# Weight differences made ahead of the join, all low halves of the last projection on VectorE, and a new order of its seven products

## What is computed

```
def conv_glu_ffn(h_norm, w_in, conv_w, conv_b, w_out):
    gate, up = jnp.split(h_norm @ w_in, 2, axis=-1)
    S = gate.shape[1]
    padded = jnp.pad(gate, ((0, 0), (CONV_WIDTH - 1, 0), (0, 0)))
    conv = conv_b
    for t in range(CONV_WIDTH):
        conv = conv + padded[:, t:t + S, :] * conv_w[t]
    return (jax.nn.silu(conv) * up) @ w_out
...
        h = h + conv_glu_ffn(rms_norm(h, norm_ffn[l]), w_ffn_in[l], ffn_conv_w[l], ffn_conv_b[l], w_ffn_out[l])
```

## Time and profile before

| | us |
|---|---|
| median of 3 runs (lowest, highest) | 1416.52 (1416.09, 1418.0) |
| the profiled execution: its time, and its span | 1415.03, 1413.3 |
| PE busy of the span | 1388.4 (98%) |
| DVE, POOL, ACT busy | 879.0, 666.3, 648.7 |
| mean granted clock of TensorE | 0.998 of full speed |

### The profile page before, as it was taken

The page is one execution under the profiler, slowest core; times in us unless marked ns, Lnnn a source line. Parts: engine busy times, 40 slices in busy tenths (PEclk is TensorE's granted clock), DMA queues, the critical chain, the costliest instruction groups (busy, mean ns, idle before and its releaser), DMA issues.

```text
span 1413.3 us, 17598 instructions
## 1 busy us (share of the span) xinstructions
PE 1388.4 (98%) x6797; PEld 1135.6 (80%) x6797; DVE 879.0 (62%) x1249; ACT 648.7 (46%) x1109; POOL 666.3 (47%) x365
## 2 busy tenths in 40 slices
PE   8999999999999999999999999999999999999998
PEld 6888778887788888888888887788777878887886
DVE  4584674665776206663265656836658895888687
ACT  6747583665332212322346555735753333334333
POOL 5645663542444344444346367535344434443542
PEclk9999999999999999999999999999999999999999
DMA  6332012331233233333333210223223602530521
GB/s 175 98 99 64 27 46 75 113 111 50 86 104 105 97 92 104 96 90 98 96 90 103 86 61 16 76 71 109 90 66 91 209 24 60 181 117 1 157 67 59
DMA packets 176305, 125.67 MB, mean 89 GB/s; under 512 B 14657, under 2 KB 152672, under 8 KB 176224
## 3 DMA queue, kind: packets, MB, share of 16 engines
q1 hardware_dynamic: 175664, 124.55, 29.4%
q10 hardware_dynamic: 560, 0.01, 0.0%
HBM read 122.44 MB, written 2.10 MB: 88 GB/s over the span
## 4 chain that ended last, share of the span: by engine, by line
PE 88%; DVE 8%; ACT 1%; issue 1%; DMA 1%; SPq 0%; DVEq 0%; ACTq 0%
PE bank L751 25%; PE bank L755 25%; PE bank L753 25%; PE bank L925 2%; DVE h L1912 1%; PE bank L1054 1%; PE bank L1055 1%; PE bank L1134 1%; PE bank L913 1%; PE bank L1094 1%; DVE w_lo L1919 1%; DMA raw<-in_w_ffn_in 1%; DVE Q L2108 1%; PE bank L1209 1%; DVE h_tok L1886 1%
## 5 line engine op out<-in xcount | busy, mean ns | idle before, releaser
L674 POOL TENSOR_TENSOR w_lo<-raw,w_hi 128x1024 fp32r<-128x1024 f32 (+2 forms) x206 | 495.0, 2408 | 596.0 <-ACT w_hi L1334 594.2
L751 PE MATMUL bank<-x_hi,w_hi 128*128 128x512 f32 x944 | 371.5, 394 | 3.8 <-issue 2.5
L755 PE MATMUL bank<-x_hi,w_lo 128*128 128x512 f32 x944 | 367.6, 389 | 0.0
L753 PE MATMUL bank<-x_lo,w_hi 128*128 128x512 f32 x944 | 367.5, 389 | 0.0
L1334 ACT ACTIVATE w_hi<-raw 128x1024 fp32r<-128x1024 f32 (+2 forms) x205 | 212.9, 1040 | 245.4 <-PE bank L755 236.9
L751 PEld LDWEIGHTS bank<-x_hi,w_hi 128*128 128x128 f32 x944 | 177.3, 188 | 47.2 <-issue 7.8
L753 PEld LDWEIGHTS bank<-x_lo,w_hi 128*128 128x128 f32 x944 | 177.3, 188 | 37.6 <-issue 1.4
L755 PEld LDWEIGHTS bank<-x_hi,w_lo 128*128 128x128 f32 x944 | 177.2, 188 | 36.9
L2226 DVE SCALAR_TENSOR_TENSOR conv<-gate_in,gains_all,conv 128x512 f32<-128x512 f32 x44 | 113.4, 2577 | 1.6
L1685 ACT ACTIVATE conv_silu<-conv 128x512 f32<-128x512 f32 x44 | 27.8, 632 | 176.5 <-DVE conv L2227 176.5
L1867 DVE TENSOR_TENSOR h<-h,bank 128x512 f32<-128x512 f32 x48 | 31.8, 681 | 105.3 <-PE bank L755 105.2
(11 more groups left out here) (341 smaller groups left out, 2484.8 us busy)
## 6 DMA issues: line engine op xcount, KB each, us to landing
raw<-in_w_ffn_in SPq DMA_DIRECT2D x88, 512.0 KB, 3.9
raw<-in_w_in SPq DMA_DIRECT2D x27, 512.0 KB, 3.7
raw<-in_w_ffn_out SPq DMA_DIRECT2D x20, 512.0 KB, 3.6
raw<-in_w_mix_out SPq DMA_DIRECT2D x16, 512.0 KB, 3.8
raw<-in_w_ca_kv SPq DMA_DIRECT2D x32, 256.0 KB, 3.2
raw<-in_w_ca_q SPq DMA_DIRECT2D x8, 512.0 KB, 3.4
raw<-in_w_ca_out SPq DMA_DIRECT2D x8, 512.0 KB, 3.9
raw<-in_w_in SPq DMA_DIRECT2D x12, 256.0 KB, 2.9
```

What stands on the lines that cost most here:

```text
L674: pool.tensor_tensor(w_lo[gi % SPLIT][:, c0:n], whole[:, c0:n], w_hi[gi % SPLIT][:, c0:n].bitcast(f32), ALU.subtract).then_inc(S["lo_split ...
L751: pe.matmul(o, ah, bh, start=first, stop=False, skip_group_check=shared_bank)
L753: pe.matmul(o, ah, bl, start=False, stop=False, skip_group_check=shared_bank)
L755: mm = pe.matmul(o, al, bh, start=False, stop=last, skip_group_check=shared_bank)
```

## The change

Seven edits, all in the last layer's feed-forward part:

1. The products' order becomes a11·b11, a12·b21, s2·t2, s1·t1, s3·t3, s4·b22, a22·t4.
2. SiLU is made in place (`conv` onto itself) and so is `up_s` (in `act`), which frees 8 KB. A sixth home `b_u` takes t2; t4 moves from `b_t` to `b_x`. No home of a block is then rewritten by a difference before that block's own use, except by t3 in `b_y` and t4 in `b_x`.
3. t1, t2, t3 are made after chunks 4, 5, 6 of group 0 (3, 4, 5 of group 1; 2, 3, 4 of group 2), and the first slab of t4 after the last but one chunk (`T_CHUNK`).
4. The low halves of b11, b21 and b22 move from POOL to DVE: 18 instructions. The two of b11 stand after the last but one chunk and, as `between`, inside the last chunk, ahead of its "up"; the two of b21 stand after the last chunk's a12 and a22.
5. `out_stage` is a plain loop: add product q, low halves of product q+2.
6. The blocks' loads move forward (`B_LOADS`): in group 0 to the "up" slabs of chunks 2, 3, 4 and the gate of chunk 6; in groups 1 and 2 to the slabs of chunks 1 to 3. They wait for `r_bc_done` (that of this layer part) where they waited for `hk_evac`, and in later groups for the last low half that used the home.
7. Product a12·b21 takes the banks `W_BANKS`, and s1·t1 takes `Z_BANKS`.

```diff
-    PRODUCTS = (("a11", "b11"), ("s1", "t1"), ("s2", "t2"), ("a12", "b21"), ("s3", "t3"), ("s4", "b22"), ("a22", "t4"))
+    PRODUCTS = (("a11", "b11"), ("a12", "b21"), ("s2", "t2"), ("s1", "t1"), ("s3", "t3"), ("s4", "b22"), ("a22", "t4"))
...
+    B_LOADS = ((("up", 3), ("up", 4), ("up", 2), ("gate", 6)), (("gate", 1), ("up", 1), ("gate", 2), ("gate", 3)))
+    T_CHUNK = ({4: "t1", 5: "t2", 6: "t3"}, {3: "t1", 4: "t2", 5: "t3"}, {2: "t1", 3: "t2", 4: "t3"})
...
-        B_HOME = {"b11": b_x, "b12": b_y, "b22": b_z, "b21": b_v, "t1": b_t, "t2": b_x, "t3": b_y, "t4": b_t}
+        B_HOME = {"b11": b_x, "b12": b_y, "b22": b_z, "b21": b_v, "t1": b_t, "t2": b_u, "t3": b_y, "t4": b_x}
...
-                    if g == 0:
+                    if g:
+                        last_use = {"b12": 4, "b22": 5, "b11": 6, "b21": 6}[name]
+                        sp.wait_ge(S["out_lo"], out_los[slab_of(LAST, ("out", g - 1, last_use, pair_slabs(g - 1)[-1][0]))])
+                    elif name == "b21":
                         sp.wait_ge(S["hk_evac"], 2 * NT)
                     else:
-                        sp.wait_ge(S["t_lo"], t_count(g - 1, "t4", pair_slabs(g - 1)[-1][0]))
-                        sp.wait_ge(S["lo_split"], pool_los[slab_of(LAST, ("out", g - 1, 5, pair_slabs(g - 1)[-1][0]))])
+                        sp.wait_ge(S["r_bc_done"], past(LAST, "r_bc_done") + 2)
...
-                                for j, name in enumerate(B_NAMES):
-                                    at = ("gate", "up")[j % 2], g, LG[g] - 2 + j // 2
-                                    if g:
-                                        at = "gate", g, LG[g] - 4 + j
-                                    if i == layer_at[LAST][at]:
+                                for name, at in zip(("b12", "b22", "b11", "b21"), B_LOADS[g > 0]):
+                                    if i == layer_at[LAST][at[0], g, at[1]]:
                                         out_weights(g, name)
...
                         if c == LG[g] - 1:
-                            t_low(g, 1, 0, pair_slabs(g)[0][1])
+                            for s, nk in pair_slabs(g):
+                                out_low(g, 1, s, nk)
...
                         some = pair_slabs(g)
-                        each = lambda f, x: [f(g, x, s, nk) for s, nk in some]
-                        each(t_sum, "t2")
...
-                        add_product(g, 5)
-                        add_product(g, 6)
+                        for q in range(len(PRODUCTS)):
+                            add_product(g, q)
+                            if q + 2 < len(PRODUCTS):
+                                for s, nk in some:
+                                    out_low(g, q + 2, s, nk)
+                            if q == 0:
+                                for s, nk in some[1:]:
+                                    t_sum(g, "t4", s, nk)
...
+                            between()
                             dve.wait_ge(S["ffn_mm"], past(layer, "ffn_mm") + 2 * n + 2)
-                            link(dve.tensor_tensor(up_s[n % 2][:, :], pb[b + 1][:, :], r_bc[:, :], ALU.mult))
+                            link(dve.tensor_tensor(act[n % 2][:, :], pb[b + 1][:, :], r_bc[:, :], ALU.mult))
                             dve.wait_ge(S["silu_done"], past(layer, "silu_done") + 2 * n + 2)
-                            dve.tensor_tensor(act[n % 2][:, :], conv_silu[n % 2][:, :], up_s[n % 2][:, :], ALU.mult).then_inc(S["act_ready"], 1)
+                            dve.tensor_tensor(act[n % 2][:, :], cv[:, :], act[n % 2][:, :], ALU.mult).then_inc(S["act_ready"], 1)
...
+                                if c < LG[g] - 1:
+                                    glu_chunk(n, 2 * (n % 2))
+                                else:
+                                    glu_chunk(n, 2 * (n % 2), second_slab_low)
                                 pair_operands(g, c)
+                                if c in T_CHUNK[g]:
+                                    for s, nk in some:
+                                        t_sum(g, T_CHUNK[g][c], s, nk)
                                 if c == LG[g] - 2:
-                                    for s, nk in pair_slabs(g):
-                                        t_sum(g, "t1", s, nk)
+                                    out_low(g, 0, *some[0])
+                                    t_sum(g, "t4", *some[0])
                             out_stage(g)
```

More of the change, by code:

```diff
@@ L342, in build_trunk @@
         conv = [place(f"conv{i}", 93 + 2 * i, [P, SEQ]) for i in range(2)]
-        conv_silu = [place(f"conv_silu{i}", 97 + 2 * i, [P, SEQ]) for i in range(2)]
-        up_s = [place(f"up_s{i}", 101 + 2 * i, [P, SEQ]) for i in range(2)]
-        act = [place(f"act{i}", 105 + 2 * i, [P, SEQ]) for i in range(2)]
+        act = [place(f"act{i}", 97 + 2 * i, [P, SEQ]) for i in range(2)]
         PAIRS, TOKS = max(LG) // 2, SEQ // 2
@@ L350, in build_trunk @@
         p_lo = place("p_lo", 60, [P, PAIRS, len(A_AT), TOKS], f32r)
-        s_tmp = place("s_tmp", 109, [P, 4, TOKS])
-        b_x = place("b_x", 113, [P, PAIRS, HALF])
+        s_tmp = place("s_tmp", 101, [P, 4, TOKS])
+        b_u, b_x = place("b_u", 105, [P, PAIRS, HALF]), place("b_x", 113, [P, PAIRS, HALF])
         b_y, b_z = place("b_y", 137, [P, PAIRS, HALF]), place("b_z", 145, [P, PAIRS, HALF])
         b_v, b_t = h[:, 0:PAIRS, :], h[:, PAIRS:2 * PAIRS, :]
-        B_HOME = {"b11": b_x, "b12": b_y, "b22": b_z, "b21": b_v, "t1": b_t, "t2": b_x, "t3": b_y, "t4": b_t}
+        B_HOME = {"b11": b_x, "b12": b_y, "b22": b_z, "b21": b_v, "t1": b_t, "t2": b_u, "t3": b_y, "t4": b_x}
         def b_slab(name, s, nk):
@@ L568, in _ @@
                             small_rows()
-                for q, t0, half in ((3, 0, 0), (4, 2, 1), (5, 0, 1), (6, 2, 0)):
+                for q, t0, half in ((1, 0, 0), (4, 2, 1), (5, 0, 1), (6, 2, 0)):
                     for i in range(2):
@@ L1684, in silu_of_chunk @@
                         act_.wait_ge(S["silu_done"], past(layer, "silu_done") + 2 * n + 1)
-                        act_.activation(conv_silu[n % 2][:, :], conv[n % 2][:, :], ACT.Silu).then_inc(S["silu_done"], 1)
+                        act_.activation(conv[n % 2][:, :], conv[n % 2][:, :], ACT.Silu).then_inc(S["silu_done"], 1)
                     def pair_high_halves(g, c):
@@ L1895, in t_sum @@
                             b_ready(g, "b12")
-                            if g and s < len(pair_slabs(g - 1)):
-                                dve.wait_ge(S["t_lo"], t_los[slab_of(layer, ("out", g - 1, 6, s))])
+                            if g == 0:
+                                dve.wait_ge(S["hk_evac"], 2 * NT)
                             plus, minus = "b12", "b11"
@@ L1900, in t_sum @@
                             b_ready(g, "b22")
-                            dve.wait_ge(S["lo_split"], pool_los[slab_of(layer, ("out", g, 0, s))])
                             dve.wait_ge(S["t_done"], t_count(g, "t1", s))
@@ L1908, in t_sum @@
                             b_ready(g, "b21")
-                            dve.wait_ge(S["t_lo"], t_los[slab_of(layer, ("out", g, 1, s))])
+                            dve.wait_ge(S["out_lo"], out_los[slab_of(layer, ("out", g, 0, s))])
                             dve.wait_ge(S["t_done"], t_count(g, "t2", s))
@@ L2213, in _, with glu_chunk @@
                     dve.wait_ge(S["r_bc_done"], past(layer, "r_bc_done") + 2)
-                    def glu_chunk(n, b):
+                    def glu_chunk(n, b, between=lambda: None):
                             gi, cv = gate_in[n % 2], conv[n % 2]
@@ L2237, in _, with second_slab_low @@
                                 n = LG_FIRST[g] + c
[L2238 removed]
+                                some = pair_slabs(g)
+                                def second_slab_low():
+                                    for s, nk in some[1:]:
+                                        out_low(g, 0, s, nk)
+                                if c < LG[g] - 1:
+                                    glu_chunk(n, 2 * (n % 2))
+                                else:
+                                    glu_chunk(n, 2 * (n % 2), second_slab_low)
                                 pair_operands(g, c)
+                                if c in T_CHUNK[g]:
+                                    for s, nk in some:
+                                        t_sum(g, T_CHUNK[g][c], s, nk)
                                 if c == LG[g] - 2:
[L2241 to L2242 removed]
+                                    out_low(g, 0, *some[0])
+                                    t_sum(g, "t4", *some[0])
                             out_stage(g)
```

38 lines of the change are left out of this document (10 added, 28 removed).

## The result

The changed kernel takes 1424.5 us (median; 1422.24 to 1425.88), the kernel before, timed beside it, 1416.3 (1415.41 to 1418.0). The ratio is 1.0052, with a 95% interval of 1.0037 to 1.0067: slower by 5.2 to 9.5 us, 7.4 at the middle. The profiled execution took 1424.92, its span is 1422.9, 9.6 more than before. The two profiled executions thus lie just above the upper end of what the ratio of all runs allows; the traces are used to place the loss, the ratio to size it. The prediction was 1421.5, slower by 5.0. The time lies in its range and on its side. Its largest term held, and the other had the wrong sign.

A forecast was written before the change was run, and what follows sets the result against it. PE, busy 98% of the span, was taken as the bound, so only its gaps count. +7.0 (start) - 2.0 (joins) = +5.0 on 1415.03 gave 1420.0, plus 1.5 to the median: 1421.5 us; range 1413 to 1428.

The forecast's parts named there:

- The start, +7.0: Group 0's loads: b11's megabyte delays chunk 2's up slab; PE waits at chunk 3's gate, 5.5 us plus 1.6 of clock.
- The first gap: PE's wait at chunk 2's "up" for `act` of chunk 0, forecast as 0.8 us.
- Rival C: Group 0's load is hidden: the slab lands within 3.9 us; 1417.3, or 1415 with PE slack; chance 0.15.
- The joins, -2.0: Three product stretches, with sums moved ahead of them: losses of 4.9, 3.0 and 2.6, together 10.5 against 12.5 us.
- The rule weighed: DVE and POOL in SBUF: whichever starts first locks the shared ports for a whole instruction; earlier rows showed it once, the opposite once.
- rival B: At the joins DVE keeps the ports through its chains; joins lose only 3; 1414.0, or 1413.0 with the start at +6; chance 0.15.
- D: The joins get dearer: gaps above 2 us with the clock's drop in each group; 1428.5; chance 0.15.
- three conditions: Wrong if the slab lands by 1071, PE's wait is under 3 us, or the product stretches lose less than 8 us.
- B and C together: DVE keeps the ports at the joins and the start's load is hidden; about 1408.5; chance 0.05.
- the upper bound: For the joins: one gap beyond 2 us with its clock per group, 5.8 each, 17.5 in all, +5.0.
- Low halves from POOL to DVE, 0: 18 low halves give DVE 20 us more work, with room during products; 0 beyond the joins.
- order and banks, 0: The new product order and banks: a12·b21 needs no s operands; the effect is counted in the joins, nothing added.

The follow-up runs named there:

- e1: The changed kernel with b11's loads of group 0 ahead of chunk 3's gate slab instead of chunk 2's up slab; 1418.77 us, ratio 1.0006.
- e5: The changed kernel, its loads kept, with t3 behind the second product's additions, t4 behind the third's, t1 and t2 two chunks apart; 1413.34 us, ratio 0.9978.
- e4: On top of e1, t3 made behind the second product's additions, t4 behind the third's, t1 and t2 two chunks apart; 1406.16 us, ratio 0.9927.
- e2: The kernel before, with only SP's wait for `r_bc_done` added ahead of the load of chunk 2's up slab; 1417.5 us, ratio 1.0012.
- e9: On top of e8, the low halves of b21 and b22 made on POOL again; 1405.54 us, ratio 0.9939.
- e8: e4 with the order of products and their banks as in the kernel before; 1405.29 us, ratio 0.9922.
- e6: On top of e1, b11's low halves made on POOL again instead of DVE; 1428.88 us, ratio 1.0087.
- e3: On top of e1, both slabs of t4 made in the product stretch, none in the last chunk but one; 1413.43 us, ratio 0.9982.

## Why the prediction was right, point by point

**The sum.** Slower by 5.0 was forecast, 7.4 was measured. The side was earned by one term, the start. That the time fell into the range is in part its width, 15 us: the traces put the start 0.6 and the joins 4.2 above their forecasts, and the second miss is nearly as large as the whole forecast.

**The start, +7.0.** Held, in place and in size: the trace gives 7.6 (gap 4.6, clock 3.0), e1 6.5 and e5 against e4 7.2. The slab's high half came at 1073.38, where I had 1074.0 from the later sequence of the same loads; `act` of chunk 0 ended at 1077.46 (1078.4), and chunk 3's gate started at 1088.71 (1089.6). All are 0.6 to 0.9 early. The first gap, 0.8 us at chunk 2's "up", did not open here (0.1), because `act` was ready as PE's turn came; in e5, with the same loads, it was 0.6. The clock was undersized: 1.6 was taken from the earlier trace rows, where it was low for a part of 4 us, and here it was low over 13 matmuls and the restart, which is 3.0. The two errors cancel, which is luck. Rival C, a hidden load, would have needed the slab 3.9 us after its issue. e2 shows that case: it is what happens without the megabyte.

**The joins, -2.0: the step that failed.** They cost +2.2 in the trace, and e1, where the start is as before, is 0.9 us above the kernel before (-0.4 to 2.3), 0.5 by the column from `r_bc`, not 2.0 below. The mechanism was the one that I walked: DVE behind, PE waiting for b11's second and b21's first slab. In group 1, the only group that I walked, it gave 4.9, and 5.4 was measured (last gate 0.8 late, where I had 1.6; the first product 0.3; b11's second slab 2.3 and not 1.0; b21's first 1.6 against 1.7). What failed is the sentence that carried this to the other two groups, "gaps of about 2.5 and restarts, 3.0 against 5.3" for group 0 and "2.6 against 4.1" for group 2. They lost 4.6 and 4.7; without the lower clock, which e1 did not have behind the same gap, group 2 would have lost 3.0. All three groups end alike: DVE reads the last gate 6.6, 6.9 and 4.6 us after PE is done with it, and the low halves stand behind that. In groups 0 and 1 b11's second slab is the late one (2.34 and 2.31); in group 2, with its shorter products, it is b21's first (2.93).

Inside the walk one assumption was too mild and one too harsh. I let POOL put one low half between the sums of a pair (4.6 us); in two of group 1's three pairs it put one ahead of each (6.8). In turn POOL was then done before the convolution, whose first instruction took 0.55 and not the 1.6 of the earlier trace rows.

**The rule weighed.** The rows of the change above show it four times: in the pairs of 1132.58, 1239.19 and 1264.86 POOL had begun 0.22 us before DVE, and DVE's sums waited for it; in that of 1251.01 DVE began first, kept its first sum at 1.2, and lost the second. This is what the Trainium skill, page "SBUF — State Buffer", section "SBUF: two separate sides", says (whichever engine starts first locks the other out), and the trace agrees with it in all four. The pair at 1156.76 in the earlier trace rows, on which rival B leaned, did not stand alone, though: the kernel before shows the same once more, in group 1, POOL and then DVE:

```profile
1285.00 3.67 POOL L674 TENSOR_TENSOR w_lo<-h,w_hi 128x1024 fp32r<-128x1024 f32 x1 [15.31 <-ACT w_hi L1334]
...
1285.19 1.22 DVE L1919 TENSOR_TENSOR w_lo<-b_x,w_hi 128x1024 fp32r<-128x1024 f32 x1
```

POOL is recorded first by 0.21 and 0.19 us in these two, by 0.22 in the three of the change, and the outcome is the opposite. So a lead of 0.2 us in the recorded starts does not tell which engine goes first, and what does stays open. No pair of sums in the change went DVE's way like this.

**Rivals.** B needed DVE to keep the ports in its chains; pairs of 6.75 refute it. D, gaps above 2 us in each group, came half true: the gaps were there (2.34, 2.31, 2.93), the clock fell after one only. None of the three conditions under which I was to be wrong was met: the slab landed at 1073, the wait was 5.5, the stretches lost 13.3. Three sums of the rivals do not come out as written. B's three pairs and 2.3 behind them, 9.2 against 5.4 of idle time, leave DVE 3.8 late and not one or two; B and C together give 1409.8 from their own terms and not 1408.5; and the 5.8 for each group in the upper bound is 0.5 above the 5.3 that group 0 lost.

**Low halves from POOL to DVE, 0; order and banks, 0.** Nothing contradicts either (e9, e8), but both were tested only where the joins are cheap. One correction: keeping b11's on DVE is not neutral but a gain, since on POOL they cost 10 to 11 us (e6).

## What to carry to other kernels

A load that waits on a semaphore holds back every transfer behind it in its queue, so look at the slab right behind the new wait and ask who reads it, and when. Work that is made ahead of a join to relieve it must fit into the idle time of the engine that makes it; what does not fit comes back at the join, here nearly one for one (3.4 us of 3.6 in e3), and the work is better placed just behind the join, in a stretch where that engine waits for PE. When two engines subtract in SBUF at once, look at where the other one's instructions fall, and not only at how many there are: the same pair of sums took 2.4, 4.6 or 6.8 us here.
